# RWKV core: the chunk inverse held as 32x32 diagonal blocks, widened by ScalarE before its one full product

## What is computed

```python
def step(S, inp):
    r_t, w_t, k_t, v_t, a_t, b_t = inp
    sa = jnp.einsum('bhij,bhj->bhi', S, a_t)
    S = S * w_t[:, :, None, :] + sa[..., None] * b_t[:, :, None, :] + v_t[..., None] * k_t[:, :, None, :]
    return S, jnp.einsum('bhij,bhj->bhi', S, r_t)
_, y = lax.scan(step, jnp.zeros((B, H, N, N), f32), seq)
```

## Time and profile before

| | |
|---|---|
| median of 3 executions | 2285.0 us |
| the profiled execution | 2284.82 us, its span 2283.0 us |
| TensorE busy | 2202.5 us, 96% of the span |
| VectorE, ScalarE, GpSimd busy | 1092.4, 804.8, 467.9 us |
| chain that ended last, TensorE's share | 85%, of it L1634 6% |
| granted TensorE clock, mean | 0.975 of full |

### The profile page before, as it was taken

One profiled execution on the slowest core, in us unless ns is written; L12 is line 12 of the kernel. 1 busy time (PEld: TensorE's weight loads), 2 busy tenths in 40 slices (PEclk: granted clock), 3 DMA queues, 4 the chain that ended last, 5 costly groups with the idle time before them and its releaser, 6 DMA issues.

```text
span 2283.0 us, 51042 instructions
## 1 busy us (share of the span) xinstructions
PE 2202.5 (96%) x22812; PEld 1867.3 (82%) x22812; DVE 1092.4 (48%) x1562; ACT 804.8 (35%) x1388; POOL 467.9 (20%) x595
## 2 busy tenths in 40 slices
PE   7999998999899999999999999999998999999997
PEld 6888887877699965788888888888886667888886
DVE  5433325767566555843332563333274537433323
ACT  4333313565233343533331343332142424433320
POOL 2111112420223223511110221110151204111102
PEclk9999999999999999999999999999999779999999
DMA  4323321320000012232232122232132012323311
GB/s 160 130 93 105 123 88 38 131 68 20 13 4 4 4 57 94 80 124 99 100 127 88 50 100 102 103 121 102 56 92 84 1 37 75 111 93 118 127 52 38
DMA packets 29099, 183.43 MB, mean 80 GB/s; under 512 B 3232, under 2 KB 8160, under 8 KB 9936
## 3 DMA queue, kind: packets, MB, share of 16 engines
q1 hardware_dynamic: 28032, 178.79, 22.3%
q0 software_dynamic: 848, 1.37, 0.3%
HBM read 174.31 MB, written 4.30 MB: 78 GB/s over the span
## 4 chain that ended last, share of the span: by engine, by line
PE 85%; DVE 10%; ACT 3%; POOL 1%; issue 1%; DMA 0%; SPq 0%; DVEq 0%; POOLq 0%; ACTq 0%
PE psum L289 67%; PE psum L1634 6%; DVE arena L355 2%; DVE arena L403 1%; PE psum L1625 1%; PE psum L381 1%; PE psum L2527 1%; PE psum L2526 1%; PE psum L2513 1%; PE psum L1658 1%; DVE arena L393 1%; DVE arena L331 1%; DVE split L264 1%; PE psum L2357 1%; DVE h L360 1%
## 5 line engine op out<-in xcount | busy, mean ns | idle before, releaser
L289 PE MATMUL psum<-x,split 128*128 128x256 f16 (+1 forms) x5568 | 638.7, 276 | 7.1 <-POOL x L422 5.5
L289 PEld LDWEIGHTS psum<-x,split 128*128 128x128 f16 x5568 | 542.9, 98 | 99.3 <-issue 15.1
L289 PE MATMUL psum<-x,split_more 128*128 128x256 f16 (+1 forms) x2496 | 287.1, 276 | 2.5 <-DVE x L2625 1.5
L289 PE MATMUL psum<-x,arena 128*128 128x256 f16 (+2 forms) x2448 | 281.1, 276 | 7.6 <-DVE arena L657 6.8
L725 POOL TENSOR_TENSOR arena<-arena 128x256 f16<-128x256 f32 (+1 forms) x176 | 120.4, 684 | 797.6 <-ACT arena L574 797.6
L289 PEld LDWEIGHTS psum<-x,split_more 128*128 128x128 f16 x2496 | 244.6, 98 | 39.6 <-issue 1.9
L289 PEld LDWEIGHTS psum<-x,arena 128*128 128x128 f16 (+1 forms) x2448 | 240.2, 98 | 43.1 <-DVE arena L264 7.3
L264 DVE SCALAR_TENSOR_TENSOR split<-stage,split 128x2048 f16<-128x2048 f32 (+1 forms) x77 | 189.9, 2467 | 157.4 <-ACT split L258 157.4
L289 PE MATMUL psum<-arena,split 128*128 128x256 f16 (+1 forms) x2304 | 261.6, 275 | 0.0
L289 PEld LDWEIGHTS psum<-arena,split 128*128 128x128 f16 x2304 | 225.4, 98 | 35.0 <-issue 2.5
L652 DVE SCALAR_TENSOR_TENSOR arena<-psum,arena 128x256 f32<-128x256 f32 (+1 forms) x176 | 75.5, 429 | 311.1 <-ACT arena L568 306.4
(11 more groups left out here) (220 smaller groups left out, 2601.6 us busy)
## 6 DMA issues: line engine op xcount, KB each, us to landing
stage<-in_w_gu SPq DMA_DIRECT2D x88, 1024.0 KB, 4.9
stage<-in_w_down SPq DMA_DIRECT2D x32, 1408.0 KB, 6.1
stage<-in_w_rkv SPq DMA_DIRECT2D x12, 1024.0 KB, 5.0
stage<-in_w_out SPq DMA_DIRECT2D x4, 1024.0 KB, 4.7
stage<-in_w_q SPq DMA_DIRECT2D x4, 1024.0 KB, 4.8
stage<-in_w_o SPq DMA_DIRECT2D x4, 1024.0 KB, 5.7
h_spill<-h SPq DMA_DIRECT2D x1, 2112.0 KB, 12.0
out<-h SPq DMA_DIRECT2D x8, 256.0 KB, 2.1
```

The lines of the kernel that those rows point to most:

```text
L289: last = pe.matmul(o, wt(wp, k), xs(xp, k), start=(k == 0 and wp == 0 and xp == 0), stop=(k == tiles - 1 and wp == 1))
```

## The change

U, X and the turned inverse are held as diagonal blocks alone: buffers of 32 columns a pair in place of 64, 256 columns in all. The turned inverse in this form is XB; the wide XT stays for the SA product. `product` at levels 2 to 5 becomes `blocks`: 16 matmuls of 32x32 with 32 columns for each half where there were 8 of 64x64 with 64 columns. `narrow` takes 128 columns of a bank. GpSimd builds XB from the even and the odd columns in four operations of 256 columns, with one more wait, and clears both XT once after chunk 0's masks. Level 6 reads and writes the narrow forms; VectorE copies its corner into the wide XT. ScalarE widens XB into XT by four copies of 32 partitions (`widen`), two between the copies of R0 and R1 and two after `copy_u(6)`; `state_sa` waits for the last of them.

```diff
...
-for _n, _w in [("ident", P), ("ones", P), ("heads", P), ("eye", HD), ("m1", HD), ("m1T", HD)] + \
+for _n, _w in [("ident", P), ("ones", P), ("heads", P), ("eye", HD), ("eye32", 32), ("m1T", HD)] + \
...
-    SA, stn, U, R = (buf(spf, k * N) for k in (4, 5, 6, 7))
-    X = (buf(spf, 8 * N), buf(spf, 9 * N))
+    SA, stn, R = (buf(spf, k * N) for k in (4, 5, 7))
+    U = buf(spf, 6 * N, 32)
+    odd = buf(spf, 6 * N + N // 2, 32)
+    X = (buf(spf, 8 * N, 32), buf(spf, 8 * N + N // 2, 32))
+    XB = (buf(spf, 9 * N, 32), buf(spf, 9 * N + N // 2, 32))
...
-    i_pool = Steps(sem("start_pool"), ["XTm", "XT"] + [f"N{l}" for l in levels])
+    i_pool = Steps(sem("start_pool"), ["even", "odd", "XTm", "XT"] + [f"N{l}" for l in levels])
...
+    xt_pool, xt_act = sem("inverse_cleared"), sem("inverse_widened")
     def after(e, s, name, i):
...
     def wide(name, n=PAIRS // 2):
-        return c(name).unsqueeze(1).to_broadcast([P, n, HD])
+        return c(name).unsqueeze(1).to_broadcast([P, n, CST[name][1]])
+    def block(b):
+        return slice(32 * b, 32 * b + 32), slice(32 * (b % 2), 32 * (b % 2) + 32)
...
     def bank(n, f):
+    def narrow(n, f):
+        return psum[:, BANK[n][f], 0:N // 4].rearrange("p (q t) -> p q t", q=PAIRS // 2)
     def bank2(n, f):
...
+        def blocks(o, f, a, b, wide_a):
+            for q in range(4):
+                for z in range(4):
+                    r, t = block(z)
+                    last = e.matmul(o[r, q, :], a[r, 4 * f + q, t] if wide_a else a[r, 4 * f + q, :],
+                                    b[r, 4 * f + q, :], start=True, stop=True)
+            return last
         def corner(o, f, turned, x, xt, nt):
-            lo, hi = slice(0, 32), slice(32, 64)
+            hi = slice(32, 64)
-                        last = e.matmul(o[low, q, hi], U[high, 4 * f + q, lo], xt[high, 4 * f + q, hi],
+                        last = e.matmul(o[low, q, :], U[high, 4 * f + q, :], xt[high, 4 * f + q, :],
-                        last = e.matmul(o[high, q, lo], nt[low, 4 * f + q, hi], x[low, 4 * f + q, lo],
+                        last = e.matmul(o[high, q, :], nt[low, 4 * f + q, hi], x[low, 4 * f + q, :],
...
-                    last = product(bank("U", f), f, (Nk[l], X[n % 2]))
+                    last = blocks(narrow("U", f), f, Nk[l], X[n % 2], True)
-                    last = corner(bank("U", f), f, False, X[n % 2], XT[n % 2], first(bs[n % 2]))
+                    last = corner(narrow("U", f), f, False, X[n % 2], XB[n % 2], first(bs[n % 2]))
         def across(l, n):
...
-                    last = product(bank("T", f), f, (U, XT[n % 2]))
+                    last = blocks(narrow("T", f), f, U, XB[n % 2], False)
-                    last = corner(bank("T", f), f, True, X[n % 2], XT[n % 2], first(bs[n % 2]))
+                    last = corner(narrow("T", f), f, True, X[n % 2], XB[n % 2], first(bs[n % 2]))
         def state_r(i):
...
         def state_sa(i):
-                after(e, l_dve, f"T6_{f}" if i else f"T4_{f}", i)
+                e.wait_ge(xt_act, i + 1)
+                if i:
+                    after(e, l_dve, f"T6_{f}", i)
         def state_s(i):
...
-                    ins = e.activation(hf(U, f), bank("U", f), ACT.Copy)
+                    ins = e.activation(hf(U, f), narrow("U", f), ACT.Copy)
-                        ins = e.activation(hf(U, f)[p0:p0 + 32, :, 0:32], bank("U", f)[p0:p0 + 32, :, 0:32],
-                                           ACT.Copy)
+                        ins = e.activation(hf(U, f)[p0:p0 + 32], narrow("U", f)[p0:p0 + 32], ACT.Copy)
-        def copy_state(name, dst, i):
-            for f in range(2):
+        def widen(n, z):
+            if z == 0:
+                e.wait_ge(xt_pool, 1)
+                after(e, l_dve, "T5_1" if n else "T4_1", n)
+            r, t = block(z)
+            ins = e.activation(XT[n % 2][r, :, t], XB[n % 2][r, :, :], ACT.Copy)
+            if z == 3:
+                ins.then_inc(xt_act, 1)
+        def copy_state(name, dst, i, halves_of=(0, 1)):
+            for f in halves_of:
...
-            copy_state("R", R, n)
+            copy_state("R", R, n, (0,))
+            widen(n, 0)
+            widen(n, 1)
+            copy_state("R", R, n, (1,))
+            widen(n, 2)
+            widen(n, 3)
...
         def start(m):
-                e.transpose(hf2(X[m % 2], f), hf2(XT[m % 2], f)).then_inc(i_dve.sem, i_dve.step(f"X{f}"))
+                e.transpose(hf2(X[m % 2], f), hf2(XB[m % 2], f)).then_inc(i_dve.sem, i_dve.step(f"X{f}"))
         def grow(l, n):
-                xt = hf(XT[n % 2], f)
+                xb, got = hf(XB[n % 2], f), narrow("T", f)
-                    e.tensor_tensor(xt, xt, bank("T", f), ALU.add).then_inc(
-                        l_dve.sem, 2 if f == 0 else 8)
+                    e.tensor_tensor(xb, xb, got, ALU.add).then_inc(l_dve.sem, 2 if f == 0 else 8)
-                    e.tensor_tensor(xt, xt, bank("T", f), ALU.add).then_inc(l_dve.sem, l_dve.step(f"T{l}_{f}"))
+                    e.tensor_tensor(xb, xb, got, ALU.add).then_inc(l_dve.sem, l_dve.step(f"T{l}_{f}"))
-                    e.transpose(hf2(X[n % 2], f), hf2(XT[n % 2], f)).then_inc(
+                    e.transpose(hf2(X[n % 2], f), hf2(XB[n % 2], f)).then_inc(
+                    e.wait_ge(xt_pool, 1)
-                        x = xt[p0:p0 + 32, :, 32:64]
-                        ins = e.tensor_tensor(x, x, bank("T", f)[p0:p0 + 32, :, 32:64], ALU.add)
+                        ins = e.tensor_copy(hf(XT[n % 2], f)[p0:p0 + 32, :, 32:64], got[p0:p0 + 32])
         def state(i):
...
     def pool(e):
-            nt, xt = first(bs[m % 2]), XT[m % 2]
+            nt, xb = first(bs[m % 2]), XB[m % 2]
-            e.tensor_tensor(xt, nt, wide("m1T", PAIRS), ALU.mult).then_inc(i_pool.sem, i_pool.step("XTm"))
+            one = wide("m1T", PAIRS)
+            e.tensor_tensor(xb, nt[:, :, 0:32], one[:, :, 0:32], ALU.mult).then_inc(i_pool.sem, i_pool.step("even"))
+            e.tensor_tensor(odd, nt[:, :, 32:64], one[:, :, 32:64], ALU.mult).then_inc(i_pool.sem, i_pool.step("odd"))
+            e.wait_ge(i_pool.sem, i_pool.count("odd", m))
+            e.tensor_tensor(xb, xb, odd, ALU.add).then_inc(i_pool.sem, i_pool.step("XTm"))
-            e.tensor_tensor(xt, xt, wide("eye", PAIRS), ALU.add).then_inc(i_pool.sem, i_pool.step("XT"))
+            e.tensor_tensor(xb, xb, wide("eye32", PAIRS), ALU.add).then_inc(i_pool.sem, i_pool.step("XT"))
+            if m == 0:
+                e.memset(cbf[:, N:3 * N], 0.0).then_inc(xt_pool, 1)
     def outputs_ready(e):
...
     def level(k):
-    put("m1", two(level(1)))
+    put("eye32", np.tile(np.eye(32), (4, 1)))
```

## The result

The kernel after takes 2328.4 us (median of 4 runs, 2326.6 to 2333.2), the kernel before 2286.1 beside it (2281.9 to 2288.4): a ratio of 1.018, 95% interval 1.017 to 1.020. It is 42 us slower, where 2277 us was forecast, with a range of 2268 to 2303. The profiled execution spans 2325.8 us, 42.8 more than that of before.

A forecast was written before the change was run, and what follows sets the result against it. The prediction took TensorE's list of work to bound each round. Its terms came to -13 us, with +5.5 us for falls of the clock: net -7.5 from 2284.8, so 2277 us, range 2268 to 2303 (8 in 10).

The forecast's parts named there:

- A round is bound by TensorE's list: Full rounds: 24.27 or 24.28 us each, with TensorE busy 23.5 to 23.7 of it, so its work sets the time.
- all of it on TensorE's list and so on the path: Block products, levels 2 to 5: the 3.4 us saved a round shorten the round in full.
- if the small tiles' burst runs out of records: A sign that the prediction is wrong: TensorE lacks records to run during a burst of 32x32 matmuls.
- Rival 3: Block products: only two tiles run at once, or one record per 16 ns at best; 0.51 us a half, 2303 us, chance 0.15.
- Rival 4: Block products: every start costs a floor of 25 ns, 0.8 us a half, +58 us in all, 2343 us; chance 0.05.
- The block products: Levels 2 to 5: four 32x32 tiles side by side, a half 0.26 us instead of 0.467, saving 3.4 us a round.
- Tile-size changes: TensorE between 64x64 and 32x32: 0.25 us there and back, six more a round, 1.5 us added (bounds 1.1 and 2.0).
- Copies and adds: ScalarE's and VectorE's level operations get shorter; 0.24 us exposed ahead of across 2, 0.06 more than now.
- The widening: ScalarE's four copies, about 0.42 us each; two delay R1's copy and across 6 by 0.3 us a round (bounds 0 and 0.8).
- GpSimd: Building XB: four operations of 792 ns, 0.7 us later; covered in full rounds, +0.7 us in round 0.
- The sum: A full round: -3.4 + 1.5 + 0.06 + 0.3 = -1.5 us, to 22.7; all rounds together -13 us.
- The clock: Granted clock falls at the round's end in four of eight rounds, 1.5 us each; +5.5 us after 0.5 hidden in waits.

The follow-up runs named there:

- run 9: The kernel after, with every block product that gives U made twice, 256 matmuls and 256 weight loads a round more: 2398.5 us, ratio 1.050.
- run 140: Not a follow-up run: "run" is a verb here; the densest stretches of the kernel before execute 140 matmuls in 4.0 us.
- run 2: The kernel after, with only two of the four 32x32 blocks of every pair multiplied in levels 2 to 5: 2282.2 us, ratio 0.998.

## Why the prediction was wrong, by its own steps

**The step that failed** is the first: "A round is bound by TensorE's list", with only the engine's own time in view, and so "all of it on TensorE's list and so on the path" for the saving. The list has a second length, in instructions. The kernel before has 1491 a round, which need 21.7 us at 14.6 ns, under its 24.3: the limit is there and doesn't show. The change adds 512 instructions to a list with room for some 170. At a packet each 3.7 us, 14.6 ns an instruction, its 2003 need 29.2 us, whatever the engine saves: 4.9 us over before, 39 for eight rounds, and 2283.0 + 39 = 2322, against a span of 2325.8. This price is read from the kernel after itself; run 9, for which the code theory had 36.3 us beforehand and which took 37.1, gives 14.7. It is an average and no hard floor: the densest stretches of before run 140 matmuls in 4.0 us, 14.3 ns an instruction, which 64x64 tiles ask for by themselves. No row of before gives the limit. But the count of instructions and the queue of code packets stood on its page, and neither was read. The prediction's last sign of being wrong, "if the small tiles' burst runs out of records", is what the timeline shows, nine of 64 and then nothing; it had neither a price nor a chance.

**Rival 3** (2303) came nearest in kind and had the wrong mechanism. It asked whether TensorE can take records faster than one in 16 ns; in a burst it can, as the full run of 64 shows:
```profile
722.39 0.75 PE L1655 MATMUL psum<-split 32*32 32x32 f32 x64
```
(0.75 - 0.19) / 63 = 8.9 ns a start. The limit is over hundreds of instructions, not within one run; 29 ns for a matmul and its load is the pace of 64x64 tiles, and small tiles can't beat it for long. **Rival 4**, a floor of 25 ns a start, has the nearest number (2343 for the measured 2328) by luck, since the same row refutes it: as an average over a round the code's 29 ns for a matmul and its load lie close to it, for another reason. The Trainium skill's floor (TensorE: Matmul & The Clock Gate, Part 1, ≈25 ns from start to start) does not hold for small tiles in turn, with 8.9 ns measured.

**The block products**: 0.28 us a half where 0.26 stood, four tiles at once. Right. **Tile-size changes**: mostly 0.15 us from the last 64x64 start to the first small one and 0.12 back, as level 6 had it; two of the seven changes to small tiles in a round take 0.20, one of those back 0.3. Right in the main. The prediction says that the trace agrees with a drain: it shows the price, but in the earlier trace rows the first small matmul starts at 717.51, before the last large one ends by the profile (717.58). **Copies and adds**: the 0.24 us ahead of ScalarE's copy are 0.27 by the prediction's own times (720.30 less 720.03), too little to matter. The lengths answer; 269, 280 and 310 ns were put in:
```profile
L1908 DVE STREAM_TRANSPOSE split<-split 128x128 f32<-128x128 f32 x58 | 18.1, 312 | 2.0
L1906 DVE TENSOR_TENSOR split<-split,psum 128x128 f32<-128x128 f32 x58 | 15.6, 270 | 37.7 <-PE psum L1655 37.7
L1805 ACT ACTIVATE split<-psum 128x128 f32<-128x128 f32 x56 | 15.2, 277 | 8.3 <-PE psum L1655 7.0
L1816 ACT ACTIVATE cumsum_buf<-split 32x256 f32<-32x256 f32 x32 | 13.1, 410 | 0.4
```
Right. **The widening** is the last of these, 410 ns where 0.42 us from start to start were put in. What it delays is seen in run 2, where no hole hides it:
```profile
739.33 0.69 PE L1670 MATMUL psum<-split,stage 32*32 32x32 f32 x32
...
740.63 0.92 PE L1667 MATMUL psum<-split 32*32 32x32 f32 x26 [0.61 <-ACT split L1810]
```
From the last start of up 6 (739.83) to across 6: 0.80 us for 0.62 in the earlier trace rows, so 0.2 later, not 0.3. In the kernel after it is 0.58 to 0.67 in three of the six full rounds (707.50 to 708.12, 0.62) and 0.80 in the other three. In two of the first three TensorE stood in a hole within up 6 just before, which hid ScalarE's delay. **GpSimd** takes 727 ns for an operation, not 792, so it was too dear by 0.3 us in round 0:
```profile
L1963 POOL TENSOR_TENSOR split<-stage,cst 128x256 f32<-128x256 f32 x6 | 4.4, 727 | 128.2 <-DVE stage L1891 128.2
```

**The sum** of these steps was a full round of 22.7 us. Run 2 has the halves that the prediction put in (0.25 us), its changes, its copies and its widening, without the longer list, and takes 22.67 us in two of its rounds at full clock, 23.48 and 23.83 in the two with a hole. The match to a hundredth is luck, and the blocks it leaves out carry some of it; but it says that the engine's side was worked out about rightly and that the error lies beside it.

**The clock**: four falls of 1.5 us were put in for the full rounds. In run 2 two rounds fell, 2.9 us each, 5.8 in all, the same by chance. In the kernel after it fell in every round but one, and the one that begins at 795.37, with a mean of 0.94, takes 28.64 us, less than the 28.77 of the one at full clock: where TensorE waits for its code, a slower TensorE can cost nothing. In the others a fall goes with up to 1.4 us over that one.

## What to carry to other kernels

Cutting a matmul into smaller ones that run side by side saves engine time and costs instructions. In an unrolled stretch count TensorE's instructions (two for each matmul) and hold them against its time: below about 14.6 ns each, as measured here, the supply of code is the bound, and saved engine time comes back as holes that the trace ascribes to "issue". Where small matmuls are already at 29 ns each, only a change that needs fewer of them can win much; no version built here beat the kernel before with its whole result.

## What the runs showed of the hardware

- Code for TensorE comes in 16 KB packets of 256 instructions; one in 3.7 us was the sustained pace over rounds (2003 in 29.2 us, 2515 in 37.1 us; single packets 3.3 to 4.2 us apart in the kernel after), with up to 2.0 us of idle time at the blocks' ends when the list runs faster, 2.4 in run 9.
- A block starts 1.2 to 1.6 us after its packet has landed (71 holes in three kernels), and the next packet sets out some 1.2 us after that and travels for 0.9 to 1.5 us.
- Matmuls on four 32x32 tiles in turn start each 8.9 ns, on two each 16.2; on 64x64 tiles each 29 ns, with 64 moving columns or with 32.
- Waits of TensorE that need their own instructions cost 70 ns each (256 more a round) and 92 ns (512 more), with the fall of the clock that went with them; one that rides on a matmul costs nothing that shows (ratio 1.000, 0.999 to 1.001).
- A round in which the granted clock fell for a time took 1.4 to 6.2 us more when TensorE's own work is the bound (24.14 to 25.54 and 28.35, 22.67 to 25.56, 31.06 to 37.25), and 0 to 1.4 more where its code is.
